# The feed-forward's down product computed by seven block products instead of eight, with the work around it rearranged

## The reference

```python
def conv_glu_ffn(h, w_up, conv_w, conv_b, w_down):
    u = causal_dwconv(h @ w_up, conv_w) + conv_b
    a, b = jnp.split(u, 2, axis=-1)
    return (jax.nn.silu(a) * b) @ w_down
...
    y = memory_cross_attention(rmsnorm(h, g[2]), rmsnorm(mem, mem_norm_g[l]), ...)
    h = h + rmsnorm(y, g[3])
    y = conv_glu_ffn(rmsnorm(h, g[4]), ffn_w_up[l], ffn_conv_w[l], ffn_conv_b[l], ffn_w_down[l])
    h = h + rmsnorm(y, g[5])
...
    h = rms_norm(x, norm_g[layer]) * (1.0 + scale) + shift
    proj = h @ w_in[layer]
```

## Time and profile before

| | before |
|---|---|
| median of 3 runs | 2672.86 us (2671.80 to 2674.66) |
| the profiled execution | 2677.48 us |
| its span | 2675.7 us |
| mean granted TensorE clock | 0.992 |
| PE busy | 2591.7 us, 97% |
| DVE busy | 1660.7 us, 62% |
| POOL busy | 1132.6 us, 42% |
| ACT busy | 844.6 us, 32% |
| moved by DMA | 360.25 MB, mean 135 GB/s |

### The profile page before, as it was taken

How to read it: one execution, slowest core, us unless ns; L and a number is a source line. 1 busy time by engine, 2 the same in 40 slices (tenths; PEclk the granted TensorE clock), 3 DMA queues, 4 the chain that set the end, 5 groups by cost and what they waited for, 6 DMA issues and landing times.

```text
span 2675.7 us, 33149 instructions
## 1 busy us (share of the span) xinstructions
PE 2591.7 (97%) x13218; PEld 2175.1 (81%) x13218; DVE 1660.7 (62%) x2192; ACT 844.6 (32%) x1332; POOL 1132.6 (42%) x651
## 2 busy tenths in 40 slices
PE   6999899989999999999999999999999999999998
PEld 5788788877788877888888887888888888888887
DVE  4879978765512588666674468804455565476566
ACT  4011233334223333333332436312222222243342
POOL 2433100046731648787864443764222322242364
PEclk9999999999999999999999999999999999999999
DMA  4122333325311412222245453573433342476682
GB/s 153 55 95 96 99 123 127 98 100 205 118 56 64 164 65 79 87 84 82 87 138 190 162 187 112 195 263 107 134 111 106 131 148 91 155 260 210 222 315 110
DMA packets 147381, 360.25 MB, mean 135 GB/s; under 512 B 15173, under 2 KB 51229, under 8 KB 147100
## 3 DMA queue, kind: packets, MB, share of 16 engines
q1 hardware_dynamic: 65072, 177.81, 19.7%
q10 hardware_dynamic: 82156, 180.33, 18.8%
HBM read 268.90 MB, written 89.19 MB: 134 GB/s over the span
## 4 chain that ended last, share of the span: by engine, by line
PE 90%; DVE 4%; POOL 2%; ACT 2%; issue 1%; DMA 1%; ACTq 0%; DVEq 0%; POOLq 0%
PE pp L296 32%; PE pp L2188 13%; PE pp L494 11%; PE pp L2241 9%; PE pp L278 9%; PE pp L2928 2%; PE pp L1258 2%; POOL w_lo L3627 1%; PE pp L1952 1%; PE pp L1931 1%; PE pp L1544 1%; POOL w_hi L3625 1%; PE pp L1533 1%; PE pp L1583 1%; PE pp L444 1%
## 5 line engine op out<-in xcount | busy, mean ns | idle before, releaser
L3625 POOL CAST w_hi<-w_raw 128x1024 fp32r<-128x1024 f32 x184 | 220.6, 1199 | 996.3 <-PE pp L296 674.2
L296 PE MATMUL pp<-w_hi,act_hi 128*128 128x512 f32 x1344 | 535.6, 398 | 15.8 <-POOL w_lo L3627 10.4
L296 PE MATMUL pp<-w_lo,act_hi 128*128 128x512 f32 x1344 | 524.6, 390 | 0.0
L296 PE MATMUL pp<-w_hi,act_lo 128*128 128x512 f32 x1344 | 524.4, 390 | 0.0
L3627 POOL TENSOR_TENSOR w_lo<-w_raw,w_hi 128x1024 fp32r<-128x1024 f32 x184 | 470.8, 2559 | 14.7
L296 PEld LDWEIGHTS pp<-w_hi,act_hi 128*128 128x128 f32 x1344 | 253.1, 188 | 70.8 <-POOL w_lo L3627 10.9
L296 PEld LDWEIGHTS pp<-w_hi,act_lo 128*128 128x128 f32 x1344 | 252.7, 188 | 53.4
L296 PEld LDWEIGHTS pp<-w_lo,act_hi 128*128 128x128 f32 x1344 | 253.1, 188 | 48.4
L2159 POOL TENSOR_TENSOR w_lo<-w_raw,w_hi 128x1024 fp32r<-128x1024 f32 x52 | 132.5, 2550 | 164.7 <-ACT w_hi L2153 164.6
L494 PE MATMUL pp<-act_hi,w_hi 128*128 128x512 f32 x480 | 191.7, 399 | 10.6 <-DVE act_lo L835 6.5
L494 PE MATMUL pp<-act_hi,w_lo 128*128 128x512 f32 x480 | 190.0, 396 | 0.0
(11 more groups left out here) (467 smaller groups left out, 5286.1 us busy)
## 6 DMA issues: line engine op xcount, KB each, us to landing
w_raw<-in_weights SPq DMA_DIRECT2D x314, 512.0 KB, 3.5
z_s<-hg_st ACTq DMA_DIRECT2D x52, 512.0 KB, 4.4
hid_s<-ffn_cb ACTq DMA_DIRECT2D x22, 512.0 KB, 2.6
ffn_graw<-hid_s ACTq DMA_DIRECT2D x44, 256.0 KB, 3.1
hg_qkb<-hT_s SPq DMA_DIRECT2D x16, 512.0 KB, 8.3
qkvT_s<-mixin_o ACTq DMA_DIRECT2D x12, 512.0 KB, 2.8
gdn_qkv<-qkvT_s ACTq DMA_DIRECT2D x8, 768.0 KB, 6.7
front_x<-in_x ACTq DMA_DIRECT2D x8, 512.0 KB, 5.0
```

Of the source, the lines that this page charges most:

```text
L296: last = pe.matmul(dst, a[:, k, t * P:(t + 1) * P], columns(w, j, k, 0, n), start=(k == 0 and a is high and w is w_hi), stop=(k == NK - 1 ...
L3625: pool.tensor_copy(hi, raw).then_inc(w_split, 1)
```

## The change

Hidden (A, as blocks of 512 rows by tiles of odd and even k) and w_down (B) are cut in 2x2 blocks, and the product is made as seven products of blocks in place of eight: `DOWN` lists them with their operands. A product is 11 pieces n of 4 row tiles, 3 passes and 512 columns: 12 matmuls. A half of weights holds two pieces (the last of a product one). Some products go on top of another in the same PSUM banks, after ACT has copied those out (`keep`, "s") or DVE has added them up (`join`, "u", "v", "f").

The sums T1 to T4 of w_down's blocks are made in the kernel (`DownSums`): 11 groups, each one load of 1 MB, four subtractions of 128x512, and one store of 1 MB to DRAM. Groups 0 to 5 are made by DVE in `Queries`, groups 6 to 10 by POOL in `Attention` and, in POOL's order, ahead of the second strip of `xo`. ACT issues loads and stores at places in both stages, and the last two stores at the start of `xo`, where it then waits for all of them to land, ahead of `load_gains`, as their buffers are those of `xo`'s rows.

The sums S1 to S4 of the hidden blocks are made by DVE (`hidden_sums`, 4 operations of 128x512, for each of 11 pairs of tiles) between the up product's rounds, and stored by ACT.

The low parts of the down product's weights move from POOL to DVE (`split_half`). The taps of the last tile's b side are spread over pieces 1 to 3. Norm steps of tiles 0 to 3 and their turns are spread by tables over pieces 56 to 76.

```diff
-FCHUNKS = ((0, 1, 2, 3), (4, 5, 6, 7))
-N_DOWN = len(FCHUNKS) * FG
+DOWN = (("A11", "B11"), ("A12", "B21"), ("S2", "T2"), ("S1", "T1"), ("S4", "B22"), ("S3", "T3"), ("A22", "T4"))
+DOWN_HALVES = (FG + 1) // 2
+N_DOWN = len(DOWN) * DOWN_HALVES // 2
...
+            def make(self, eng, S, k, n):
+                b11, b12, b21, b22 = (self.bufs[k % 3][:, i, :] for i in range(4))
+                eng.wait_ge(self.loaded[k % 3], self.loaded_before + 16 * (k // 3 + 1))
+                S.done(eng.tensor_tensor(b11, b12, b11, ALU.subtract), "T1")
+                S.done(eng.tensor_tensor(b12, b22, b12, ALU.subtract), "T3")
...
+            def finish(self, act):
+                self.store(act, FG - 2)
+                self.store(act, FG - 1)
+                self.landed(act)
+
+            LOADS = {4: (0,), 5: (1,), 6: (2,), 10: (3,), 11: (4,), 12: (5,)}
+            STORES = {7: 0, 8: 1, 9: 2, 13: 3, 14: 4, 15: 5}
+            LATE_LOADS = {0: (6, 7), 1: (8,), 6: (9,), 7: (10,)}
+            LATE_STORES = {4: 6, 5: 7, 6: 8}
...
+            def split_half(self, eng, m):
...
+                eng.tensor_tensor(w_lo[SLOT[q]][:, 0:n], w_raw[:, r % 2 * HALF:r % 2 * HALF + n], w_hi[SLOT[q]][:, 0:n].bitcast(F32), ALU.subtract).then_inc(w_ready, 1)
...
+            TURNS = {67: 0, 70: 1, 73: 2}
+            FIRSTS = {56: 0, 58: 1, 61: 2, 67: 3}
+            SECONDS = {60: 0, 63: 1, 69: 2, 71: 3}
+            HIGHS = {68: 0, 71: 1, 74: 2}
...
+            def hidden_sums(self, k, *names):
...
+                        M.done(tt(s1, a21, a22, ALU.add), "S1")
+                        M.done(tt(s3, a11, a21, ALU.subtract), "S3")
...
+                        M.done(tt(s2, s1, a11, ALU.subtract), "S2")
...
+                        M.done(tt(s4, a12, s2, ALU.subtract), "S4")
...
                 tlow(4)
+                hidden_sums(0, "S1", "S2")
                 conv(2, "b")
                 combine(0, "c22")
...
                     combine(i, "c22")
                     gated(r - 1)
+                    if r % 2 == 0:
+                        hidden_sums(r // 2 - 1, "S1", "S2")
...
                     combine(i, "c21")
...
+                    if k == FG - 1 and p in joins:
+                        join(p, joins[p])
...
-                N_.low(dve, 0)
+                N_.low(dve, 3)
+                join(len(DOWN) - 1, "g")
                 N_.scale(dve, 4)
-                for t in range(1, NT // 2):
-                    N_.low(dve, t)
```

More of the change, by code:

```diff
@@ L631, in __init__ @@
                 self.qT = self.buf("qT", [P, NK, T])
+                self.sums = DownSums(prev.source)
             def pe(self, pe):
@@ L661, in act, with dve, taps @@
                 R.settled(act)
+                W = self.sums
                 for j in range(NT // 2, 2 * NK):
                     keep(j)
-        def taps(dve, V, name, rnd, dst, src, w, n, bias=None, amid=None):
-            for j in range(n):
+                    if j in W.STORES:
+                        W.store(act, W.STORES[j])
+                    if j == NT // 2 + 2:
+                        after(act, R.N, "xn", NT - 1)
+                    for k in W.LOADS.get(j, ()):
+                        W.load(act, k)
+            def dve(self, dve):
+                self.sums.dve(dve)
+        def taps(dve, V, name, rnd, dst, src, w, n, bias=None, amid=None, only=None):
+            for j in range(n) if only is None else (only,):
                 k = n - 1 - j
@@ L2407, in act @@
                 first(7)
-            def keep(self, act, t):
-                c = [t in tiles for tiles in FCHUNKS].index(True)
-                after(act, self.down_made, "made", t)
-                self.kept.done(act.activation(self.y[:, t, :], pp[t - FCHUNKS[c][0]][:, :], ACT.Copy), "kept")
             def dve(self, dve):
```

371 lines of the change are left out of this document (260 added, 111 removed).

## The result

| | before | changed |
|---|---|---|
| median | 2673.76 us (6 runs, 2670.68 to 2678.71) | 2683.22 us (6 runs, 2675.60 to 2687.25) |
| ratio to before | | 1.0032, 95% interval 1.0019 to 1.0044 |
| the profiled execution, and its span | 2677.48, 2675.7 us | 2682.12, 2680.3 us |
| mean granted TensorE clock | 0.992 | 0.991 |

A forecast was written before the change was run, and what follows sets the result against it. PE was taken to bound the kernel, busy for 97% of the span. The terms summed to -10.7 us, taking the profiled 2677.5 us to 2666.8 and the forecast median to 2662.2 us, range 2648 to 2673.

The forecast's parts named there:

- 132 matmuls, -29.9, and the last pair, -1.6: Down product: 924 matmuls instead of 1056 save 29.9 us; the last pair's wait for a norm low part goes, 1.6.
- Does DVE keep up there?: Down product: DVE's low parts and weight halves stay nearly ahead of PE, costing +2 us (0 to 5).
- The stepping through: Down product, pieces 54 to 74: followed piece by piece, low parts stay ahead of PE, only join f is late.
- The join that it priced at 1.8 us: Down product: join f stands behind a `normalise` and a weight half, so PE waits 1.8 us.
- Rival 3: Down product: weight loads landing above 7.7 us slow it; at 9 us, 27 us more, 2689 us; chance 0.07.
- The prediction's own sign of this rival: Down product: PE gaps in pieces 0 to 50, with ACT's casts waiting for `w_raw`.
- Rival 2: Whole kernel: DVE becomes the bound, costs +34.5 against -31.5, 2676 us, same within the bound; chance 0.16.
- First round: Up product's first round: four sums ahead of c22 cost +7.5 us (2.7 to 8), lost clock +2.3 (0 to 4).
- nine even rounds: Up product's other even rounds: sums in DVE's gap before c21 cost 0.2 us each, +2 us (0 to 9).
- `Attention`, 0: Queries and Attention: weight sums are covered and POOL does not hold up DVE there; 0 us (0 to 3).
- Start of `xo`: Start of `xo`: the last weight sum's load, subtractions and store leave margins near zero; +1.5 us (0 to 5).
- Hand-over: Down product's end into second block: job 4 starts 34.5 us after it; +5.5 us (2 to 9).

The follow-up runs named there:

- e10: Changed kernel with z slots reordered, norm steps retimed, pair 0's sums earlier, c copies later, e9's casts, last five weight sums on VectorE: ratio 0.9913, median 2652.58 us.
- e9: Changed kernel with ScalarE's casts of the down product's half strips one piece later; ratio 0.9992 to the kernel before.
- e5: Changed kernel with weight sums 6 to 10 made by VectorE in Attention instead of by POOL; ratio 1.0015 to the kernel before.

## Why the prediction was wrong

The mechanism failed in one term above all. By its terms, the first trace's differences beside them:

- *132 matmuls, -29.9, and the last pair, -1.6*: right. e10's down product is 213.5 us, and 244.2 less 31.5 is 212.7.
- ***"Does DVE keep up there?", +2 (0 to 5)***: this is the step that failed; it was +15 us (228.0 less 212.7), of which 10.8 are waits of PE. Some 4 more are the lower clock behind them, which this term left out: without waits the stage is 217.2 us here and 213.1 in e10. The question was put as one of time: 57 us of work in 57 us. That was the wrong question. DVE was not full, as the windows of pieces 54 to 74 say, in the changed kernel and in e10 (columns as the earlier trace rows):

```profile
1540.00:1612.00 72.00, 63.33 (x277) 51.44 (x275) 52.81 (x66) 35.02 (x61) 2.40 (x1) 0.95 0.59 194
```

```profile
1527.00:1587.00 60.00, 59.56 (x276) 49.28 (x275) 53.73 (x68) 36.55 (x63) 2.77 (x1) 1.00 0.68 230
```

  DVE had 52.8 us of work in 72 us there, and 53.7 in 60 in e10, where it kept up. The stepping through had low parts always ahead of PE, and missed both waits inside its steps: that `normalise` waits for a store that had been issued just ahead of it, and that ACT's cast waits in front of the high parts and squares. The join that it priced at 1.8 us waited 4.36; the low part of piece 2, priced at 0.2, did not wait. The first of the two waits could have been read from the trace of before, where it held up nothing that PE needed (lines, DVE, 1390 to 1612):

```profile
L469 DVE SCALAR_TENSOR_TENSOR ffn_y<-ffn_y,ffn_small,mod 128x1024 f32<-128x1024 f32 x4 | 5.1, 1285 | 4.0 <-DMA x_s<-ffn_y 4.0
```

- *Rival 3, the weight loads*: it had the right object and the wrong condition. It asked that a load land in 7.7 us, so that two halves keep pace, and looked at 3.5. The loads from `dsum_s` landed in 4.5 at the median of the page, well inside, and the kernel was slower all the same. The limit was not how many loads fit, but how long ACT may stand with only two pieces, 5.4 us, of work done ahead. e9 shows it: the loads are as slow (over all of the down product's weights the median is 4.3 us, in the changed kernel 4.1), and PE's waits are gone but for the join. The prediction's own sign of this rival did appear: PE had a gap of 1.57 us at 1460.89, at piece 25, and ACT's cast had waited 6.13 us for `w_raw` until 1458.45.
- *Rival 2, DVE as the bound*: its 2676 us and rival 3's 2689 lie on either side of the 2683 measured, and neither mechanism is the one found. e10 has as much work for DVE and keeps up.
- *First round, +7.5 and +2.3; nine even rounds, +2*: the first was right in kind, 8.4 us waited where 8 to 10 were named, sums of 1.63 to 1.77 us, and 15 matmuls in the 5 us behind it. The round grew by 9.2 us where 9.8 were named: 6.7 more for c22, 0.9 more for T4's low part, and some 1.6 of clock. The stretch grew by 9.9 for 11.8: all later rounds but two took 19.0 us as before, those two 19.4, so the even rounds cost next to nothing, though most of their sums ran at 1.7 us too. The rule of the Trainium skill (SBUF — State Buffer, "Who interferes with whom"), that the two engines lock each other out, held here in size: 1.63 to 1.77 us where 0.68 is the shortest.
- *`Attention`, 0*: +2.8. The term said that operations with one operand in SBUF are not held up. `TENSOR_SCALAR` was. e5 settles it for the operations, e10 for the stretch.
- *Start of `xo`, +1.5*: no clear cost. In ten traces that have it alike it was 0.2 to 3.6 us more than in the one trace of before, 1.4 at the mean.
- *Hand-over, +5.5*: +4.0, job 4 at 33.3 us after the end where 34.5 was named. Right.
- *The z product*: not in the sum at all, so put at nothing without a reason, and +3.4. Every term had been about what the change does where it stands. The ring of slots is carried on from stage to stage, and a stage 190 us later waits by the remainder of a count.

In sum: -10.7 was forecast and +4.6 came in the profiled execution. The 15.3 between them are 13.2 in the down product, 3.4 in z, 2.8 in `Attention`, 1.3 in `xo`, less 1.9 in the up product and 1.5 in the hand-over; and chance at both ends of the span, -3.8 and +1.8. The terms' own bounds, added up, give 2646 to 2684 us and not the 2647 to 2680 of the text, so the measured 2683.2 is inside them; the range had set that end aside.

## What to carry to other kernels

When work is packed beside a bound engine, the sum of busy times says little. For each waiting instruction in an engine's order, ask how long it can stand and what of the bound engine's next inputs is queued behind it, against the distance that the engines are ahead; and put the instruction that waits for a DMA or a slot as late as its own deadline allows. A stage's cost can also come from a counter that it leaves in another position: when a change alters how many buffers of a ring are used, look at the first user after the ring is changed.
